# One tile's input pieces in order over one DMA queue, weights begun behind them, 4 KB pieces for the value weights, and 57 offsets in a scheduler's priorities

## The reference

```
xn = rmsnorm(x, g_mix_pre);  u, bg, cg, h = split(xn @ w_in)        # 1024 -> 4 x 512
y_pool = per group of 128 channels: (trailing mean over 2, 4, 8 or 16 rows - u) @ w_pool * scale
y_conv = bg * causal_conv3(cg * h)
x = x + rmsnorm([group_norm(y_pool), group_norm(y_conv)] @ w_out, g_mix_post)
m = rmsnorm(mem, g_mem);  k = m @ w_k;  v = m @ w_v                  # 256 memory tokens, 4 heads
x = x + rmsnorm(softmax(q(rmsnorm(x)) k / 16) v @ w_co, g_x_post)
x = x + rmsnorm(relu(rmsnorm(x) @ w_up)^2 @ w_down, g_ff_post)       # 1024 -> 4096 -> 1024
```

## Time and profile before

| what | value |
|---|---|
| runs of the kernel | 850.74, 848.03, 848.91 us, median 848.91 |
| the profiled execution, its own time | 847.59 us |
| its span from first to last instruction, slowest core (core 4) | 845.9 us |
| spans of the eight cores | 838.9 to 845.9 us |
| PE busy, share of the span | 806.1 us, 95% |
| DVE, ACT, POOL busy | 47%, 45%, 12% |
| granted clock of TensorE, mean of core 4 | 0.997 |
| POOL's queue (q0): bytes, share of the 16 engines' span | 68.37 MB, 46.3% |

### The profile page before, as it was taken

One profiled execution on the slowest core, in us unless ns is written; L12 is line 12 of the kernel. 1 busy time (PEld: TensorE's weight loads), 2 busy tenths in 40 slices (PEclk: granted clock), 3 DMA queues, 4 the chain that ended last, 5 costly groups with the idle time before them and its releaser, 6 DMA issues.

```text
span 845.9 us, 13457 instructions; the slowest of 8 cores (838.9 to 845.9 us)
## 1 busy us (share of the span) xinstructions
PE 806.1 (95%) x4444; PEld 386.5 (46%) x4529; DVE 398.0 (47%) x556; ACT 383.6 (45%) x799; POOL 103.3 (12%) x180
## 2 busy tenths in 40 slices
PE   2799998999999999999999999999999999999997
PEld 0444454444464454454444454444444444444443
DVE  3897965688876577656222222231122321222112
ACT  3587755847777567675331223332233411233101
POOL 5713110212012012210010000000000000000000
PEclk9999999999999999999999999999999999999999
DMA  9999499800298515995799726871248820184011
GB/s 188 192 235 199 112 178 286 133 1 1 49 161 118 181 45 181 153 174 105 143 151 171 177 75 135 153 143 50 100 104 151 155 65 26 61 148 91 1 50 51
DMA packets 26352, 103.43 MB, mean 122 GB/s; under 512 B 2402, under 2 KB 9186, under 8 KB 20268
## 3 DMA queue, kind: packets, MB, share of 16 engines
q0 software_dynamic: 15968, 68.37, 46.3%
q1 hardware_dynamic: 9740, 32.75, 11.6%
q10 hardware_dynamic: 576, 1.44, 0.6%
HBM read 146.48 MB, written 18.07 MB: 195 GB/s over the span
## 4 chain that ended last, share of the span: by engine, by line
PE 84%; DMA 9%; issue 2%; DVE 2%; ACT 2%; POOL 1%; ACTq 0%; DVEq 0%; POOLq 0%; SPq 0%
PE ps L679 82%; DMA wdn<-w_down 4%; PE ps L684 2%; DMA XT<-xt 2%; DMA x<-X 1%; DMA up<-w_up 1%; DMA X<-xp 1%; ACT rf L708 0%; DVE O L715 0%; ACT sq L708 0%; DVE X L734 0%; POOL sAB L717 0%; ACT z L708 0%; DVE sqx L715 0%; DVE pld L734 0%
## 5 line engine op out<-in xcount | busy, mean ns | idle before, releaser
L679 PE MATMUL ps<-xT,up 128*128 128x512 bf16 x1001 | 221.3, 379 | 1.3 <-issue 0.2
L679 PE MATMUL ps<-wdn,hid 128*128 128x512 bf16 x1002 | 220.8, 379 | 1.7 <-DMA wdn<-w_down 0.6
L679 PEld LDWEIGHTS ps<-wdn,hid 128*128 128x128 bf16 x1024 | 99.9, 98 | 120.2 <-issue 1.0
L679 PEld LDWEIGHTS ps<-xT,up 128*128 128x128 bf16 x1024 | 99.6, 98 | 119.5 <-issue 1.1
L715 DVE TENSOR_TENSOR O<-ps,gp 128x1024 f32<-128x1024 f32 (+1 forms) x49 | 58.6, 1201 | 186.4 <-PE ps L679 129.0
L708 ACT ACTIVATE rt<-ps 128x512 bf16<-128x512 f32 x128 | 76.4, 597 | 139.3 <-PE ps L679 131.7
L679 PE MATMUL ps<-xT,win 128*128 128x512 bf16 x500 | 119.0, 382 | 18.1 <-DMA win<-w_in 14.9
L715 DVE TENSOR_TENSOR hid<-rt 128x512 bf16<-128x512 bf16 x128 | 54.4, 425 | 150.8 <-ACT rt L708 148.9
L708 ACT ACTIVATE sqj<-ps 128x1024 bf16<-128x1024 f32 (+1 forms) x33 | 32.8, 995 | 176.2 <-PE ps L679 174.4
L679 PEld LDWEIGHTS ps<-xT,win 128*128 128x128 bf16 x512 | 49.7, 98 | 75.3 <-issue 19.0
L734 DVE SCALAR_TENSOR_TENSOR X<-O,st,X 128x1024 f32<-128x1024 f32 (+1 forms) x49 | 62.1, 1276 | 5.4 <-DVE O L715 4.7
(11 more groups left out here) (204 smaller groups left out, 678.3 us busy)
## 6 DMA issues: line engine op xcount, KB each, us to landing
up<-w_up POOLq DMA_DIRECT2D x32, 1024.0 KB, 8.6
x<-X SPq DMA_DIRECT2D x16, 512.0 KB, 5.2
X<-x SPq DMA_DIRECT2D x16, 512.0 KB, 4.3
wdn<-w_down POOLq DMA_DIRECT2D x8, 1024.0 KB, 30.3
yp<-X SPq DMA_DIRECT2D x15, 512.0 KB, 2.6
X<-xp POOLq DMA_DIRECT2D x8, 512.0 KB, 44.0
X<-xp SPq DMA_DIRECT2D x8, 512.0 KB, 6.0
win<-w_in POOLq DMA_DIRECT2D x4, 768.0 KB, 27.5
```

Of the source, the lines that this page charges most:

```text
L679: P.add([("pe", lambda e, L: e.matmul(L(out), lhsT=lhsT, rhs=rhs, start=start, stop=stop, skip_group_check=True), max(0.03, n * 0.000421 + ...
```

## The change

Four edits.

1. The four pieces of tile 0 all go over SP's queue in order, and ACT issues the constants alone. `act` now returns its operation; the Square on one column is kept as `warm`, and POOL's first loads (`win`, `xe`, `wpool`, states) are made to depend on it, so POOL's first transfer waits for it and the ones behind it follow.
2. The value weights `w_v` are laid out in HBM as four pieces of 4 KB for each partition and half, and loaded as such (before: 16 KB in a row). `w_k` stays.
3. The scheduler's picture of the start: POOL's queue moves nothing before 8.9 us (`DMA_POOL`), POOL itself is free from 2.0 (before: 6.9).
4. Functions get names with a running number (`@named`), and a table `ORDER` with 57 entries (name, engine) shifts the priority of an operation in it; a positive number is earlier.

```diff
+ORDER = {
+    ("conv_group 0", "dve"): -180, ("conv_group 12", "dve"): -70, ("conv_group 13", "act"): 340, ("conv_group 15", "dve"): 250,
...
+    ("kv_block 0", "pe"): 40, ("kv_block 1", "act"): -280, ("kv_block 1", "pe"): -250, ("kv_block 3", "pe"): -60,
...
-        op.prio = op.idx - lead
+        op.part = (self.part, opts[0][0])
+        op.prio = op.idx - lead - ORDER.get(op.part, 0)
...
+    DMA_POOL = 8.9
...
-        free = {e: 6.9 if e == "pool" else 1.0 for e in self.ENGS}
+        free = {e: 2.0 if e == "pool" else 1.0 for e in self.ENGS}
...
         def dma_next():
-            act = [e for e in self.ENGS if dq[e]]
+            act = [e for e in self.ENGS if dq[e] and (e != "pool" or dq_t[0] >= self.DMA_POOL)]
             if not act:
-                return None
+                return self.DMA_POOL if dq["pool"] else None
...
-    wk_d = din("w_k", [2, 128, 4096]); wv_d = din("w_v", [2, 128, 4096])
+    wk_d = din("w_k", [2, 128, 4096]); wv_d = din("w_v", [2, 4, 128, 1024])
...
-    act(stat(128), epsb[:, 0:1], AF.Square)
+    warm = act(stat(128), epsb[:, 0:1], AF.Square)
...
     def kv_loads(k, after=None):
-        load(wkv[k % 2][:, :], (wk_d if k < 2 else wv_d)[k % 2], 2097152, q="pool", after=after, desc=16384)
+        if k < 2:
+            load(wkv[k % 2][:, :], wk_d[k], 2097152, q="pool", after=after, desc=16384)
+        else:
+            load(r3(wkv[k % 2][:, :], 4), wv_d[k % 2].rearrange("j p c -> p j c"), 2097152, q="pool", after=after)
...
-    load_win(0)
+    load_win(0, warm)
     for i in range(4):
-        load(XT[i], xt0[i], 524288, q=("sp", "act")[i % 2])
+        load(XT[i], xt0[i], 524288)
     load_consts()
-    load_win(1)
-    load(Xe[0:NX, :], xe[:, :], NX * 4096, q="pool")
+    load_win(1, warm)
+    load(Xe[0:NX, :], xe[:, :], NX * 4096, q="pool", after=warm)
```

More of the change, by code:

```diff
@@ L674, in build_program, with named, wrap, g @@
     psum = {F32: psum_f, BF16: [p.bitcast(BF16) for p in psum_f]}
+    def named(name):
+        def wrap(fn):
+            def g(*a, **k):
+                n = P.parts.get(name, 0)
+                P.parts[name] = n + 1
+                old, P.part = P.part, "%s %d" % (name, n)
+                r = fn(*a, **k)
+                P.part = old
+                return r
+            return g
+        return wrap
     def mm(out, lhsT, rhs, start, stop, share=1):
@@ L708, in f @@
             return e.activation(out=L(out), in_=L(in_), func=func, scale=scale, **kw)
[L709 removed]
+        return P.add([("act", f, c_act(n) + (0.19 if accum is not None else 0.0) + (0.06 if bias is not None else 0.0))], reads=rdl, writes=wr, lead=lead)
     def tt(out, in0, in1, op, eng="dve", per=1.0):
@@ L794, in load_wpool @@
     def load_wpool():
-        load(wpool[:, :], wpool_d[:, :], 262144, q="pool")
+        load(wpool[:, :], wpool_d[:, :], 262144, q="pool", after=warm)
     def rstd(ss, r):
@@ L805, in build_program @@
     xs_n = [0]
+    @named("pre_sub")
     def pre_sub(X, r, gc, dst, sq_out=None):
@@ L823, in build_program @@
     late_stage = [False]
+    @named("post")
     def post(ps, X, r, gp, free_se=False):
@@ L834, in post @@
         return stt(X, Ob, rs, X, ALU.mult, ALU.add)
+    @named("post_halves")
     def post_halves(ps, X, gp, dst):
@@ L854, in build_program @@
     Xof = {}
+    @named("load_tile")
     def load_tile(t, src, lead=LEAD, q="sp"):
@@ L896, in pre_turned @@
             stt(x, x, gcs[:, kc:kc + 1], ps.v(0, 128, 0, TN), ALU.mult, ALU.mult)
+    @named("pre_first")
     def pre_first():
@@ L922, in out_tile @@
         tiles = {}
+        @named("out%d_" % t)
         def part(i, k0, k1):
@@ L959, in load_gps @@
         load(gps[:, :], gs4[k], 131072, q=q, lead=LEAD if q == "pool" else LEAD // 2)
+    @named("out_smp")
     def out_smp(chunks, nk, w):
@@ L975, in out_smp @@
         stt(Xs[:, :], Ob, rs, Xs[:, :], ALU.mult, ALU.add)
+    @named("pre_smp")
     def pre_smp(gc):
@@ L1000, in build_program @@
     wo = lambda kc, h: wout[:, kc * D + h * 512: kc * D + (h + 1) * 512]
+    @named("proj")
     def proj(chunk, rhs, n, out):
@@ L1009, in build_program @@
     WIN = [(0, 1), (1, 2), (2, 4), (4, 7), (7, 10), (10, 13), (13, 16)]
+    @named("load_win")
     def load_win(k, after=None):
@@ L1016, in us @@
         return Us[:, g * 64:(g + 1) * 64].rearrange("p (b c) -> p b c", b=2)
+    @named("windows")
     def windows(cur_ap, w, s3, width, L, pooled, first=None):
@@ L1044, in build_program @@
     sq_n = [0]
+    @named("group_rstd")
     def group_rstd(sqap, mat, width, n):
@@ L1059, in nsq @@
         return s
+    @named("pool_group")
     def pool_group(t, g):
@@ L1088, in pool_group @@
             tt(pl[:, 0:16], tmp, Ug[:, 16:32], ALU.subtract, eng="pool")
+        @named("fin_pool")
         def finish():
@@ L1098, in pool_group @@
         return finish
+    @named("conv_group")
     def conv_group(t, cc):
@@ L1122, in conv_group @@
             tt(z, z, r0[:, :], ALU.mult, eng="dve pool")
+        @named("fin_conv")
         def finish():
@@ L1129, in conv_group @@
         return finish
+    @named("ext_pool_proj")
     def ext_pool_proj():
@@ L1137, in ext_pool_proj @@
             copy(U[g][:, 0:16], ps.v(0, 128, NS, NX), eng="act")
+    @named("ext_states")
     def ext_states():
@@ L1146, in ext_states @@
         copy(Vs[:, :].rearrange("p (g b c) -> p g b c", g=4, b=2)[:, :, :, 0:2], src(32, 36), eng="act dve")
+    @named("ext_pool_rest")
     def ext_pool_rest():
@@ L1174, in build_program @@
     b2 = lambda a: a.rearrange("p (b c) -> p b c", b=2)
+    @named("ext_conv")
     def ext_conv(cc):
@@ L1191, in ext_conv @@
         tt(z, pb.v(0, 128, 0, NS), z, ALU.mult)
+    @named("ext_conv_rest")
     def ext_conv_rest():
@@ L1203, in ext_conv_rest @@
         tt(r3(mgs[:, 4 * NS:8 * NS], 4), r3(r, 4), gb, ALU.mult)
+    @named("ext_state_out")
     def ext_state_out(after):
@@ L1220, in ext_state_out @@
         dma("sp", o_conv_s[:, :], sT[32:36, :], 8192, wr=False)
+    @named("state_out")
     def state_out():
@@ L1242, in build_program @@
     mTk = lambda kc: mT[:, kc * 256:(kc + 1) * 256]
+    @named("kv_block")
     def kv_block(k):
@@ L1270, in build_program @@
     wc = lambda kc, h: wco[:, kc * D + h * 512: kc * D + (h + 1) * 512]
+    @named("fold_a")
     def fold_a(c):
@@ L1282, in fold_a @@
             copy(Am[:, c * D + g * 512: c * D + (g + 1) * 512], ps.v(0, 128, 0, 512), eng="act dve")
+    @named("fold_b")
     def fold_b(m):
@@ L1293, in build_program @@
     wb = lambda kc, h: Bm[:, kc * D + h * 512: kc * D + (h + 1) * 512]
+    @named("attn_head")
     def attn_head(t, hh):
@@ L1303, in attn_head @@
         tt(psm[hh % 2][:, :], p[:, 0:TN], p[:, TN:2 * TN], ALU.add, eng="pool")
+        @named("fin_attn")
         def finish():
@@ L1313, in attn_head @@
         return finish
+    @named("turn_blocks")
     def turn_blocks(rows, dst):
@@ L1321, in turn_blocks @@
              ps.v(0, 128, 0, 256, BF16, lambda a: a.rearrange("p (q g t) -> p g q t", q=2, g=4)), eng="act dve")
+    @named("smp_loads")
     def smp_loads():
@@ L1325, in smp_loads @@
         wload(vSs[:, :], cv, 0, 8)
+    @named("smp_q")
     def smp_q():
@@ L1335, in smp_q @@
         turn_blocks(q, qTs[:, :])
+    @named("smp_attn")
     def smp_attn():
@@ L1386, in up_chunk @@
         tt(hid(c), r, r, ALU.mult, per=0.5)
+    @named("up_smp")
     def up_smp(k):
```

30 lines of the change are left out of this document (20 added, 10 removed), and 9 rows, old and new, of the table ORDER.

## The result

The changed kernel took 841.2 us (median of 7 runs), the kernel before 850.7 in the same set of runs: ratio 0.9884, 95% interval 0.9864 to 0.9904, 9.5 us less. 843.0 (838.5 to 848.5) was predicted, 5.9 us under the 848.9 that the kernel before had then; the two times lie closer together than the two gains, because the kernel before was 1.8 us slower in this set. Each set of runs has its own median of the kernel before (848.9 to 853.6 us), so kernels of different sets are compared by their ratios.

The account below looks back on a forecast made before the run. PE, busy 95% of the span, was taken as the bound, so only its start, waits and half clock could gain. Terms left core 3 slowest at 840.1, 5.8 us less, giving 843.0 us, range 838.5 to 848.5.

Parts of the forecast that it names:

- The sum: All terms per core: core 4 6.2 us less, core 3 4.7 less; the slowest core 5.8 us less.
- Tile 2's sub-tiles: PE's `xs` stall goes through shorter stores (one value load moved, 4 KB pieces): -5.2 us on core 4, -1.2 on core 3.
- Rival B: The `xs` stall at tile 2 stays, as stores and weights still meet: 846 to 848.5 us, chance 0.17.
- The slack of 3.5 us for the load: Tile 2's second value load, started near 129 us, is needed 23 us later; the slower load took 19.4.
- Tile 1: Moving the memory half's square later removes waits: -2.2 and -1.7 (clock) on core 3, -0.8 on core 4.
- The start: Before the first output matmul: PE some 3 us earlier but then waiting for `wout`; worth 0, bounds -1.6 to +1.6.
- `V`: The 1.3 us wait for `V` at tile 2's end is halved by reordering: -0.6, bounds 0 and -1.3.
- New waits, +1.0: Unnamed new waits from 126 more places where the kind of work changes: +1.0 us, bounds 0 and 3.
- Rival D: 126 more changes of operand kind on PE each expose a weight load of about 0.1 us: 855.6 us, chance 0.06.
- A: The gain at the start counts, `wout` landing earlier through a better filled stream: 838 to 841 us, chance 0.13.
- C: `wout` lands 1.6 us later, PE idles 3 to 5 us before it, clock falls: 845 to 848, chance 0.11.

Follow-up runs that it names:

- the run with the load at 106 us: The changed kernel with one more 2 MB load of value weights, into an unread scratch tensor, issued at about 106 us: 854.25 us, ratio 1.0001.

## Why the prediction was right, and where it was off

**The sum: right in its place, too small in its size.** 5.9 us were forecast and 9.5 measured. On core 3, the slowest that was forecast and the slowest there is, 4.7 were forecast and 7.1 profiled. Its waits from the first `wout` matmul to 180 us gave 3.2 of 3.0 forecast, the half clock 3.4 of 1.7. At nothing I had put the idle time before the first `wout` matmul (1.6 less) and that behind 180 us (0.9 less), and, the other way, the first matmul (0.7 later) and PE's work (1.3 more).

**Tile 2's sub-tiles: right, in size and cause, with one cause too many.** The stall and the half clock behind it went on core 4; on core 3 0.7 of its 1.2 us is left. The cause is the moved load; "that one comes in 4 KB pieces" was no cause. Rival B took half its weight from the rule of the Trainium skill on packets, and was right that the pieces do nothing but wrong in what it made of it: the moved load alone was enough. The stores of core 4 up to 128 us came to 3.4 to 6.2 us, where 4 to 7 were expected. The slack of 3.5 us for the load was too small an estimate: on core 3 the load takes 15.1 us from 127.4, lands at 142.5, and PE's first matmul with it starts at 150.5.

**Tile 1: right in size, its cause not tested.** ACT waits 0.17 us for the memory, and PE's 2.2 us with their clock are gone on core 3. No run undid these offsets alone, so it isn't shown which of them did it.

**The start: the 0 held, its reasoning did not.** `wout` lands at 59.6 in the mean, 59.8 before: the stream sets it, as assumed, and the run without POOL's wait shows it again (loads 2.1 us earlier, and a landing 0.2 to 0.3 us before its set's others). The Trainium skill's "DMA: Bandwidth & Descriptors", section "Issuing engines are not separate DMA queues", says that the transfers of all issuing engines run on the same 16 DMA engines, and the trace now agrees. But "PE could reach its first output matmul some 3 us earlier" and so waits 1 to 4 us for `wout` failed: core 3 waits 0.8, core 4 not at all. I had read the earlier start from core 4, whose 14.9 was the latest of all; in the mean the first matmul went from 13.8 to 15.0. It starts 0.25 us behind the landing of POOL's first weights before and after, and these land at 14.7 instead of 13.5; the earlier pieces don't bear on it. The Square ended at 3.06, as worked out, but POOL issued 0.6 us behind it.

**What was left out: the step that failed.** PE idled 5.8 us before its first `wout` matmul and idles 4.0 now, which I had put down as worth nothing, since PE would only wait longer for `wout`. It didn't: the first `wout` matmul starts at 60.3 in the mean instead of 60.7, but by the account above 1.5 us more of PE's work stands ahead of it (on six cores 318 matmuls instead of 310, one sub-tile's transposes of tile 1 more), and work done in an idle stretch shortens the rest. With the idle time went a stretch at half clock near 38 us on six of the eight cores, core 3 among them, 1.7 us each. On core 3, first before, then changed:

```profile
38.20:41.60 3.40, 2.97 (x9) 0.97 (x8) 2.83 (x8) 2.97 (x7) 0.37 (x2) 0.50 0.90 281
```

```profile
38.20:41.60 3.40, 3.40 (x19) 1.55 (x17) 3.10 (x6) 3.08 (x8) 0.18 (x1) 1.00 0.94 299
```

I counted the half clock only where a long wait stood before it; here PE had waits of 0.6, 0.7 and 0.9 us, which end at 34.2, 36.7 and 38.0 us. They don't settle it: cores 2 and 4 had the same waits and stayed at full clock. Near 38 us it is absent both with the new start alone and with the table alone; with the new start alone one near 61 us took its place. These 1.7 us are the largest part of the 2.4 by which core 3 gained more than forecast.

**`V`: right.** 1.3 became 0.7.

**New waits, +1.0: too high.** From the first `wout` matmul to 180 us PE idles 1.3 us in the mean, old and new.

**Rival D: refuted.** PE's work is 809.3 us against 809.0 in the mean, for 126 more changes of kind: 2 to 3 ns each, where 47 were needed. (The pages' busy times, 806.1 and 809.7 us, look like D's sign of 3 us more, but the first is of core 4, whose trace lacks 85 of 4529 matmuls; on core 3, with all of them, it is 811.8 before and 809.7 now.) Core 3, one matmul of each kind in turn, starts 0.22 us apart:

```profile
120.37 0.38 PE L716 MATMUL ps<-wout,mg 128*128 128x512 bf16 x1
120.59 0.38 PE L716 MATMUL ps<-wkv,mT 128*128 128x512 bf16 x1
120.80 0.38 PE L716 MATMUL ps<-wout,mg 128*128 128x512 bf16 x1
```

**A and C.** On core 4 `wout` landed at 58.8, under the 59 that I gave as A's sign; the cores' landings lay 2.4 us apart before, and one core couldn't carry that bound. In the mean it moved by 0.2 us, so neither A nor C.

**Open.** The two `kv_block 1` offsets hold half of the gain. The other half (0.9939 to 1) is in the remaining table, since start and pieces show nothing by themselves. Which of the two offsets, which of the other 55 entries and which of the shorter waits before 61 us and at 75 to 90 us make it was not taken apart.

## What to carry to other kernels

Where rows are stored and reloaded into the same buffer, a wait of PE for a norm can be the end of a chain store, load, norm, transposes, and a large load beside the store, or beside the load behind it, stretches it. Look which weight load becomes free to issue in front of that chain, and delay what frees its buffer until the chain is through; here two numbers in an order table gave 0.6%, and a delay that was too short gave nothing (1.0012). And count PE's short waits too: idle time ahead of a late transfer isn't worthless when work from behind can be put into it, and on six of eight cores waits under 1 us were followed by the same 1.7 us at half clock as one of 3.5.

## What the runs showed of the hardware that was not expected

- The price of one 2 MB load beside 512 KB transfers of another queue isn't one number. In the run with the load held to 121 us (all eight cores), stores issued before it took 2.6 to 5.2 us and those issued behind it 10.6 to 13.9; in the changed kernel 23 stores that ran mostly beside one value load took 5.4 to 9.3. What makes the difference was not taken apart. The price in time of such a load in the wrong place was 10 us (0.9884 to 1.0001), since a store holds the next load into its buffer.
- In the run with the load at 106 us the granted clock of core 0 was 0.50 for 10.2 us. It fell 6.6 us before the wait of 9.9 us ended, and cost only where PE had work: 1.8 us on this core, 2.3 in the mean of the cores.
- The value weights in 1024 packets instead of 256 (the 768 more, at three more for each row) let the stores in no sooner: beside them a store took 9.2 to 12.1 us in the kernel before with 4 KB pieces, and 9.7 to 12.8 without.
